# Projections of a two-block transformer kernel in a new order of weight panels

## The reference

```python
h = rms_norm(x, g_attn)                       # x: 1 x 512 x 1024
z = h @ w_in
(fq, fk, fv, f_logit, nq, kc, vc, ksl, vsl, kwn, vwn, n_gate, g_a, g_b) = split(z)   # 512,512,512,8,512,6 x 128,24,1024,1024
log_f = log_sigmoid(f_logit + b_f);  c = cumsum(log_f)          # bias of the first attention ("fox")
kc = silu(blocks(kc) @ w1_k) @ w2_k;  vc = silu(blocks(vc) @ w1_v) @ w2_v   # compressed keys and values
gates = sigmoid(n_gate)                       # three gates a head for the second attention ("nsa")
```

## Time and profile before

| | us |
|---|---|
| median of 3 runs | 1747.6 (1747.34 to 1747.71) |
| the profiled execution's own time | 1747.78 |
| its span in the trace | 1746.0 |
| TensorE (PE) busy, share of the span | 1648.7, 94% |
| first matmul starts | 13.63 |
| first matmul of the attention stage starts | 183.25 |

### The profile page before, as it was taken

How to read it: one execution, slowest core, us unless ns; L and a number is a source line. 1 busy time by engine, 2 the same in 40 slices (tenths; PEclk the granted TensorE clock), 3 DMA queues, 4 the chain that set the end, 5 groups by cost and what they waited for, 6 DMA issues and landing times.

```text
span 1746.0 us, 22108 instructions
## 1 busy us (share of the span) xinstructions
PE 1648.7 (94%) x7980; PEld 1350.3 (77%) x7980; DVE 1118.8 (64%) x1764; ACT 715.6 (41%) x1231; POOL 163.9 (9%) x187
## 2 busy tenths in 40 slices
PE   6979888998999999999989999999899899999997
PEld 5867676665887888888877787888678888888886
DVE  6465588886666666663578379998665644444456
ACT  5234686565343232322344234444633432232232
POOL 0001310000030000000000990000000000000000
PEclk9989899998999999999999999999999999999998
DMA  4326751111264555542213321221242233333332
GB/s 157 95 78 188 164 120 47 40 61 37 84 240 169 169 203 180 188 164 82 81 54 121 97 73 55 61 56 55 73 126 73 86 96 96 96 96 96 97 96 96
DMA packets 49825, 185.43 MB, mean 106 GB/s; under 512 B 6912, under 2 KB 9216, under 8 KB 47312
## 3 DMA queue, kind: packets, MB, share of 16 engines
q1 hardware_dynamic: 39456, 136.76, 24.8%
q0 software_dynamic: 10288, 47.60, 9.4%
HBM read 172.23 MB, written 6.85 MB: 103 GB/s over the span
## 4 chain that ended last, share of the span: by engine, by line
PE 68%; DVE 14%; ACT 4%; issue 3%; DMA 0%; ACTq 0%; DVEq 0%; SPq 0%
PE ps L1967 17%; PE ps L1969 16%; PE ps L1968 16%; DVE w_lo L1160 1%; PE ps L2369 1%; PE ps L2370 1%; PE ps L2371 1%; PE ps L2203 1%; PE ps L2204 1%; PE ps L2205 1%; PE ps L2164 1%; ACT w_hi L648 1%; PE ps L2426 1%; PE ps L2189 1%; PE ps L2144 1%
## 5 line engine op out<-in xcount | busy, mean ns | idle before, releaser
L1967 PE MATMUL ps<-h_hi,w_hi 128*128 128x512 f32 x1024 | 408.1, 399 | 34.0 <-DVE w_lo L1183 13.6
L1969 PE MATMUL ps<-h_hi,w_lo 128*128 128x512 f32 x1024 | 401.3, 392 | 0.0
L1968 PE MATMUL ps<-h_lo,w_hi 128*128 128x512 f32 x1024 | 401.1, 392 | 0.0
L1160 DVE TENSOR_TENSOR w_lo<-raw,w_hi 128x1024 fp32r<-128x1024 f32 x169 | 213.3, 1265 | 98.2 <-ACT w_hi L648 79.5
L1967 PEld LDWEIGHTS ps<-h_hi,w_hi 128*128 128x128 f32 x1024 | 193.9, 189 | 82.6 <-DVE w_lo L1183 13.6
L1968 PEld LDWEIGHTS ps<-h_lo,w_hi 128*128 128x128 f32 x1024 | 193.9, 189 | 41.3 <-issue 2.2
L1969 PEld LDWEIGHTS ps<-h_hi,w_lo 128*128 128x128 f32 x1024 | 193.6, 189 | 40.9
L581 ACT ACTIVATE w_hi<-raw 128x1024 fp32r<-128x1024 f32 x129 | 135.5, 1051 | 170.0 <-DMA raw<-in_panels 163.8
L1967 PE MATMUL ps<-f_hi,w_hi 128*128 128x512 f32 x408 | 166.8, 409 | 0.0
L1969 PE MATMUL ps<-f_hi,w_lo 128*128 128x512 f32 x408 | 161.3, 395 | 0.0
L1968 PE MATMUL ps<-f_lo,w_hi 128*128 128x512 f32 x408 | 161.0, 395 | 0.0
...
## 6 DMA issues: line engine op xcount, KB each, us to landing
raw<-in_panels SPq DMA_DIRECT2D x252, 512.0 KB, 3.5
...
X<-in_x SPq DMA_DIRECT2D x4, 512.0 KB, 7.7
...
```

Source lines behind the costliest of these rows:

```text
L1160: dve.tensor_tensor(w_lo[:, n % RING], raw[:, n % RING], w_hi[:, n % RING].bitcast(F32), ALU.subtract)\
L1967: pe.matmul(out, w_hi[:, u, b, :], hi[:, k, :N], start=start, stop=False)
L1968: pe.matmul(out, w_hi[:, u, b, :], lo[:, k, :N], start=False, stop=False)
L1969: ins = pe.matmul(out, w_lo[:, u, b, :], hi[:, k, :N], start=False, stop=stop)
```

## The change

All 32 first panels become one group `proj` in an order given by name: compressed keys and values first (in PSUM banks 2 and 3 of their own), the fox queries and keys, then values, compression panels (`c0` to `c7`), `low` (forget columns 0 to 7 and gate columns 32 to 55 in one panel), selected and windowed keys `s0`, `s1`, their values `v4`, `v5`, and the nsa queries `n0` to `n3`. The last, `none`, is a panel of zeros that is loaded and never multiplied. The block work of the compressed tensors is cut into pieces, one for each step (`BETWEEN`). x is loaded in five parts, the first of 256 KB; the square sums follow the split of h instead of alternating with it; activation tables are touched early. `blk_raw` is L1231's instruction, `blk_place` L1236's two, `blk_low` L1240's, `proj_low` the low part.

```diff
-GROUPS = [("fox_qk", 8), ("fox_v", 4), ("nsa_a", 4), ("mix", 16), ("gate", 16), ("branch", 8),
+GROUPS = [("proj", 32), ("gate", 16), ("branch", 8),
           ("out", 8)]
 for _c in range(4):
     GROUPS += [(f"ff1_{_c}", 8), (f"ff2_{_c}", 8)]
...
+PROJ = ["kc", "vc", "q0", "q1", "q2", "q3", "k0", "k1", "k2", "k3", "c0", "v0", "v1", "c1", "v2", "v3", "c2", "low",
+        "s0", "c3", "s1", "v4", "c4", "v5", "n0", "c5", "n1", "c6", "n2", "c7", "n3", "none"]
+AT = {name: n for n, name in enumerate(PROJ)}
+EVAC = [name for name in PROJ[2:] if name[0] in "qkvsn" and name != "none" or name == "low"]
+ORDER = {name: e for e, name in enumerate(EVAC)}
+SPLITS = [name for name in EVAC if name[0] in "qksn"]
+BANK = {name: e % 2 for e, name in enumerate(EVAC)}
+BANK.update({"kc": 2, "vc": 3, "n2": 4, "n3": 5})
+TMP_OF = {name: BANK[name] for name in EVAC}
+TMP_OF["n2"] = 1
+TURN_AFTER = {"v1": 0, "v2": 1, "v3": 2, "low": 3, "v5": 4, "n0": 5}
+NONE = AT["none"]
...
+    zf = place("zf", [8, T], F32, x_at)
+    gate_v = place("gate_v", [24, T], F32, x_at + T)
+    sig_n = place("sig_n", [24, T], F32, x_at + 2 * T)
+    nq_v = place("nq_v", [P, T], F32, cmp_at)
...
-        for f in range(4):
-            sp.dma_start(X[:, 2 * f:2 * f + 2, :], a["x"][:, 2 * f:2 * f + 2, :]).then_inc(in_x[f], 16)
-            if f == 0:
+        for n, (f, g) in enumerate(X_PARTS):
+            sp.dma_start(X[:, f:g, :], a["x"][:, f:g, :]).then_inc(in_x[n], 16)
...
-                gp.wait_ge(used, done(BASE["mix"] + 15))
+                gp.wait_ge(used, done(AT["c7"]))
...
+        def first_hi(m):
+
+            act.wait_ge(landed[m], 16)
+            act.activation(w_hi[:, m], raw[:, m], ACT.Copy).then_inc(hi_ready, 1)
+
+        act.wait_ge(setup, 1)
+        act.activation(row_max[:, 0, 0:1], p_cmp[0][:, 0, 0:1], ACT.Copy)
         act.wait_ge(in_v, 16)
         for f in range(KT):
-            act.wait_ge(in_x[f // 2], 16)
+            act.wait_ge(in_x[X_PART_OF[f]], 16)
             act.activation(h_hi[:, f, :], X[:, f, :], ACT.Copy, scale=vcol("g_attn", f)).then_inc(n_hi, 1)
+            if f == 0:
+                first_hi(0)
+        first_hi(1)
+        for f in range(KT):
             act.wait_ge(n_acc, f - 1) if f > 1 else None
             act.activation(tmp_v[:, f % 2, :], X[:, f, :], ACT.Square).then_inc(n_sq, 1)
-            if f in (2, 7):
-                m = 0 if f == 2 else 1
-                act.wait_ge(landed[m], 16)
-                act.activation(w_hi[:, m], raw[:, m], ACT.Copy).then_inc(hi_ready, 1)
-        panel_hi(2)
+            if f == 3:
+                first_hi(2)
+        first_hi(3)
         act.wait_ge(in_c, 16)
+        act.activation(row_max[:, 0, 0:1], eps, ACT.Sqrt)
...
+        for n, name in enumerate(PROJ[2:], 2):
+            if n + AHEAD == NONE + 1:
+                act.wait_ge(landed[NONE % RING], 16 * (NONE // RING + 1))
+                act.sem_inc(hi_ready, 1)
+            if n + AHEAD != NONE:
+                panel_hi(n + AHEAD)
+            if name == "n3":
+                act.wait_ge(sem("nsa_q_low"), 2)
+                fox_bias(0)
+                cmp_sums(1)
+            if name in SPLITS:
+                proj_high(name)
+            if name in TURN_AFTER:
+                v_out(TURN_AFTER[name])
+            if name == "k0":
+                blk_high(0)
+            if name == "v2":
+                blk_high(1)
+            if name == "k3":
+                act.activation(cst_r[:, 0:P], cst[:, C_ID:C_ID + P], ACT.Copy).then_inc(setup, 1)
+                act.activation(cst_r[:, P:2 * P], cst[:, C_MASK:C_MASK + P], ACT.Copy).then_inc(setup, 1)
+            if name == "low":
+                act.wait_ge(sem("forget_z"), 1)
+                chain(act.activation(lf_a[:], zf[:], ACT.Abs))
+                chain(act.activation(lf_a[:], lf_a[:], ACT.Exp, scale=-1.0))
+                act.activation(lf_a[:], lf_a[:], ACT.Ln, bias=cst[0:8, C_ONE:C_ONE + 1]).then_inc(sem("forget_ln"), 1)
+                act.wait_ge(sem("proj_val"), ORDER["low"] + 1)
+                act.activation(sig_n[:], gate_v[:], ACT.Sigmoid).then_inc(sem("gate_n"), 1)
+            if name == "s1":
+                cmp_sums(0)
+            if name == "c4":
+                cmp_hidden(0)
+            if name == "c5":
+                act.wait_ge(sem("cmp_k_out"), 1)
+                act.activation(kc_hi[:], ps[:, 6, P:P + 2 * CW].rearrange("p (g c) -> p g c", g=2), ACT.Copy)\
+                   .then_inc(sem("kc_hi_done"), 1)
...
+            if f == 3:
+                panel_lo(2)
+        panel_lo(3)
...
+        def proj_value(name):
+
+            dve.wait_ge(used, done(AT[name]))
+            dve.tensor_tensor(tmp_of(name), ps[:, BANK[name], :], rs1[:], ALU.mult).then_inc(sem("proj_val"), 1)
...
+        BETWEEN = {"q0": lambda: blk_raw(0, 0), "q1": lambda: blk_raw(0, 1), "q2": lambda: blk_raw(0, 2),
+                   "q3": lambda: blk_raw(0, 3), "k0": lambda: blk_place(0), "k1": lambda: blk_low(0),
+                   "k2": lambda: blk_raw(1, 0), "k3": lambda: blk_raw(1, 1), "v0": lambda: blk_raw(1, 2),
+                   "v1": lambda: blk_raw(1, 3), "v2": lambda: blk_place(1), "v3": lambda: blk_low(1)}
+
+        for n, name in enumerate(PROJ[2:NONE], 2):
+            if n + AHEAD == NONE + 1:
+                panel_lo(NONE + 1, also=1)
+            elif n + AHEAD != NONE:
+                panel_lo(n + AHEAD)
+            if name == "low":
+                dve.wait_ge(used, done(n))
+                dve.tensor_tensor(zf[:], ps[0:8, BANK[name], :], rs1[0:8, :], ALU.mult).then_inc(sem("forget_val"), 1)
+                dve.tensor_tensor(gate_v[:], ps[32:56, BANK[name], :], rs1[32:56, :], ALU.mult).then_inc(sem("proj_val"), 1)
+                dve.wait_ge(sem("forget_val"), 1)
                 dve.tensor_scalar(zf[:], zf[:], bf[:, 0:1], None, ALU.add).then_inc(sem("forget_z"), 1)
+            elif name in EVAC:
+                proj_value(name)
+            if name in BETWEEN:
+                BETWEEN[name]()
+            if name in SPLITS and name != "n3":
+                proj_low(name)
+            if name in TURN_AFTER:
+                v_out(TURN_AFTER[name])
...
+            if name == "s0":
                 dve.wait_ge(sem("forget_z"), 1)
                 dve.wait_ge(sem("forget_ln"), 1)
                 chain(dve.scalar_tensor_tensor(zf[:], zf[:], 0.0, lf_a[:], ALU.min, ALU.subtract))
                 chain(dve.tensor_scalar(zf[:], zf[:], -S8, None, ALU.mult))
                 chain(dve.memset(lf_a[:], 1.0))
                 dve.tensor_tensor_scan(cum[:], lf_a[:], zf[:], 0.0, ALU.mult, ALU.add).then_inc(sem("c_summed"), 1)
...
+            if name == "v4":
                 dve.wait_ge(sem("c_turned"), 1)
                 dve.tensor_scalar(c_q8[:], ps[:, 4, 0:32].rearrange("p (t h) -> p t h", h=8), -1.0, None, ALU.mult)\
                    .then_inc(sem("c_q_ready"), 1)
...
                 dve.wait_ge(sem("gate_turned"), 1)
                 dve.tensor_copy(gate_t[:], ps[:, 5, 0:96].rearrange("p (t h) -> p t h", h=24)).then_inc(sem("gate_t_ready"), 1)
...
+            if name == "n1":
                 dve.wait_ge(sem("kc_hi_done"), 1)
                 dve.tensor_tensor(kc_lo[:], ps[:, 6, P:P + 2 * CW].rearrange("p (g c) -> p g c", g=2), kc_hi[:].bitcast(F32),
-                                  ALU.subtract)
...
+                proj_low("n3")
+                panel_lo(BASE["gate"] + 1)
...
+        def project(n, out, ready=False, inside=None):
+
+            pe.wait_ge(lo_ready, n + 1)
+            for k in range(KT):
+                if ready:
+                    pe.wait_ge(n_lo, k + 1)
+                hi, lo = w_hi[:, n % RING, k, :], w_lo[:, n % RING, k, :]
+                pe.matmul(out, hi, h_hi[:, k, :], start=k == 0, stop=False, skip_group_check=True)
+                pe.matmul(out, hi, h_lo[:, k, :], start=False, stop=False, skip_group_check=True)
+                ins = pe.matmul(out, lo, h_hi[:, k, :], start=False, stop=k == KT - 1, skip_group_check=True)
+                if inside is not None and k == 2:
+                    inside()
+            ins.then_inc(used, 1)
+
+        def first_sum():
+
+            pe.wait_ge(in_c, 16)
+            pe.wait_ge(n_acc, KT)
+            pe.matmul(ps[:, 4, :], ones, sq_acc[:], start=True, stop=True, skip_group_check=True).then_inc(n_sum, 1)
...
+        for n, name in enumerate(PROJ[:NONE]):
+            if name[0] == "c":
                 compress(n)
             else:
-                panel(n // RING, n % RING, "mix", ps[:, r % 2, :], ALL, h_hi, h_lo, free=free)
...
+            if name == "q1":
+                rel_table()
+            if name in TURN_AFTER:
+                turn_v(TURN_AFTER[name])
+            if name == "s1":
+                turn_c()
+                turn_gate()
+            if name == "v4":
                 fold(0)
+            if name == "n0":
...
+                pe.wait_ge(bank_free, n + 2) if g else None
```

(69 more changed lines are left out.)

255 lines of the change are left out of this document (79 added, 176 removed).

## The result

| us | before | after | change |
|---|---|---|---|
| median of the runs shown together | 1747.65 (4 runs, 1747.34 to 1749.61) | 1728.55 (4 runs, 1725.58 to 1731.71) | -19.1 |
| profiled span | 1746.0 | 1729.9 | -16.1 |

The ratio of after to before is 0.9884, 95% interval [0.9866, 0.9902]; the forecast was 1729.3. The profiled execution (1731.71 us) is the slowest of the four, so its trace shows 3 us less gain than the median.

A forecast was written before the change was run, and what follows sets the result against it. TensorE, busy 94% of the span, was taken as the bound. The terms summed to -18.3 us, from the profiled 1747.78 to 1729.5, or 1729.3 as median; own range 1723 to 1734, with rivals 1720 to 1739.

The forecast's parts named there:

- one panel less: Projections: `low` replaces two panels and `none` has no matmuls, so 24 matmuls fewer on TensorE's path, -5.5 us.
- the start: First matmul moves from 13.63 to 9.9 us, needing only the first split and the panel's landing: -3.7 us.
- block work spread: Compressed tensors' VectorE work split over full-panel steps: the waits of 7.2 and 0.7 and 2.6 of clock go, -10.5 us.
- forget and gate, new wait: Before `s1`, TensorE waits 3.8 us behind ScalarE's table loads and panel rounding, plus 2.0 of clock: +5.8 us.
- w2 close behind: After `v5`, w2 is loaded nearer its use; `w2v` lands late and TensorE waits: +0.9 us (0 to 4).
- the tail: Before `n2`, a load slowed by POOL's burst again makes a wait near 2.9 and 1.7 behind it: 0 change.
- into the attention: At `fold(1)`, wait falls from 2.9 to 1.5 us and half of 3.3 lost clock returns: -3.0 us.
- everything later moves as it stands: After the first attention step, the gain stays whole because no load there is tied to wall-clock time: 0 change.
- Rival 4: Attention stage: the shift is lost waiting for VectorE, giving 1732.3 us; chance 0.71 jointly with the forecast.
- rival 1: Before `s1`, w2 and at the tail: the new waits stay away, 11.3 us faster, 1718.0 us; chance 0.13.
- 2: Tail: the ring starves, three loads of 8.6 us instead of one, +9.4, giving 1738.7 us; chance 0.12.
- Rival 3: Tail: store and bias starve the ring worse; at loads of 13 us, 22.4 more, 1751.7 us; chance 0.04.

The follow-up runs named there:

- e7: Changed kernel with the empty panel rounded and multiplied too, 24 matmuls more: 1731.13 us, ratio 0.99.
- e9: Changed kernel with the old start (x in four parts, squares alternating with splits, first panel rounded later, no early table loads): 1730.03 us, ratio 0.9902.
- e4: Changed kernel with the block work in two lumps, keys' in step k0 and values' in step v2: 1733.42 us, ratio 0.9919.
- e2: Changed kernel with ScalarE rounding s1's panel ahead of the forget and gate activations: 1726.83 us, ratio 0.9881.
- e1: The changed kernel run again, unedited; base of the later comparisons: 1727.13 us, ratio 0.9885.
- e5: Changed kernel with only head 0's 320 KB store to scratch_r moved early, behind the rows of r: 1721.81 us, ratio 0.9841.
- e6: Changed kernel with ScalarE's and VectorE's panel rounding ahead of the forget chain, and two turns moved behind v4: 1723.39 us, ratio 0.9853.
- e10: e8 with head 1's store to scratch_r also moved early, beside head 0's: 1719.22 us, ratio 0.9835.
- e8: Changed kernel with the edits of e5 and e6 together: 1717.78 us, ratio 0.9821.
- e3: Changed kernel with all eight 320 KB stores to scratch_r issued early, near 46 us: 1752.51 us, ratio 1.0027.

## Why the prediction was right, by its steps

| term | forecast | measured |
|---|---|---|
| one panel less | -5.5 | 4.9 by trace at `w2v`, 4.0 in medians (e7) |
| the start | -3.7 | 13.63 to 10.17: -3.5; undone alone +2.9 (e9) |
| block work spread | -10.5 | all its waits gone; lumped again, in other places, +6.3 (e4) |
| forget and gate, old waits | -2.3 | gone |
| forget and gate, new wait | +5.8 (3.8 + 2.0) | wait 3.99; from 112.21 to the turn 8.5, 3.0 over a panel |
| w2 close behind | +0.9 | 0 |
| the tail | 0 | wait 4.09 for 2.93, panel 7.1 as 7.2: +1.2 |
| into the attention | -3.0 | wait 0.63 for 2.9; first step 6.05 for 8.48: -4.7 |

The panel and the waits that are gone counted in full, the terms add up to -5.5 - 3.5 - 10.5 - 2.3 + 7.0 + 0 + 1.2 - 4.7 = -18.3 by the `w2v` product; the trace has 18.7 there (191.7 to 173.0). That this is the forecast's own sum is in part luck: the tail and the new wait came out 2.4 dearer, the attention and w2 2.6 cheaper. And the forecast let everything later move as it stands, which it does not (see "Later").

*Start.* Forecast 9.9, measured 10.17, 9.96 and 9.81. The reciprocal was forecast to end at 29.9 and ended at 31.0, and no bank waited for it; VectorE kept up through all eight query and key panels.

*The new wait before `s1`* was forecast at 3.8 and came as 3.99, 3.97 and 3.99, by the chain named: three table loads, the Sigmoid, then `w_hi`. The added clause, that a running sum would fill the time if the clock were full, is what e2 shows: without the wait TensorE stood 1.94 for `cum` and 0.47 for `w_lo`. *On the tables, the Trainium skill ("ScalarE: Activation LUTs", "What ACT_TABLE_LOAD costs") adds a drain of some 1380 ns to each load of 1283 ns; the rows of after have loads of 1.28 us with the next activation 0.01 to 0.02 behind each, and the wait is 3.99, not the 3.8 + 4.1 that an estimate from the page's figures would give.*

*The price of a wait.* The forecast added 2.0 of clock to a wait of 3.8 and 1.7 to one of 2.9. Measured behind `s1`'s wait: 3.0 in the first trace, 1.7 in e1 (110.70 to the turn at 117.94), 3.1 in e5; behind `n2`'s wait 1.6 and 1.7 in the first two, 2.7 in e2, e4 and e6. So the same wait in the same kernel cost 1.7 in one execution and 3.0 in another. Waits of 2.4 together (e2) and of 2.0 (e10) were each followed by 1.7; the wait of 1.9 for `gate_z` in the first attention head was followed by matmuls of 0.63 us before and of 0.39 after. Behind waits up to 0.8 us (e8) the granted clock stayed 1.00.

*w2.* The forecast took 5.2 us for `w2v` to land and a wait of 0.9; the load took 3.6 in after, and there was no wait. Ahead of the store it stands in both kernels; but before, SyncE issued a panel load 0.3 us behind it, and after, the next panel load comes 4.8 us behind. That this is what made the 5.2 was not tested.

*Tail and attention.* The wait before `n2` was put at 2.9 for a load of 8.6; the load took 9.7 and the wait was 4.09. The forecast blamed the burst as a whole; e5 shows that it is the one store. The step into the attention was sized too small: with 0.63 the wait fell under those that keep the clock, so all of the loss there went, not half.

*Later.* Of the 18.7, 16.1 were left at the end of the first trace, and this step of the prediction ("everything later moves as it stands") is wrong by 1.4 us. These go at the start of group `out`, where TensorE waits for the reloaded X. The reload in the kernel before, in the changed one and in e7, and TensorE's wait in the changed one:

```profile
X<-in_x POOLq DMA_DIRECT2D x1, 2048.0 KB, 8.2
...
X<-in_x POOLq DMA_DIRECT2D x1, 2048.0 KB, 9.7
...
X<-in_x POOLq DMA_DIRECT2D x1, 2048.0 KB, 8.3
...
472.45 0.47 PE L1996 MATMUL ps<-h_hi,w_hi 128*128 128x512 f32 x1 [1.29 <-DVE X L1468]
```

It is no chance: in all ten traces with one panel less the load takes 9.4 to 9.8 us and TensorE waits 1.07 to 1.39; in the kernel before and in e7, which has the extra panel, it takes 8.2 and 8.3 and there is no wait. So it goes with the panel less, which brings 4.9 to 5.5 at its place and 4.0 at the end. Why the load takes longer there stays open. The other loss of the first trace, 1.1 near the second block's first norm (granted clock 0.50 from 880 to 885 us, 1.00 in e1), did not come again: of the other ten traces seven win 1.5 to 1.8 there on the one of the kernel before, which has a slow stretch of its own at that place (granted clock 0.80 from 900 to 905 us), and three win nothing. So in e1 21.8 were won at `w2v`, 20.3 near 830 us and 22.3 at the end. Rival 4 (a loss in the attention stage) did not hold: from the `w2v` product to group `out` no trace differs from the kernel before by more than 1.7 us, in both directions.

*Rivals.* 1 was wrong: the waits before `s1` and `n2` came. Take both away, as e8 does, and the kernel runs 1717.8, where rival 1 said 1718.0; that is close in part by luck, since its 11.3 holds 0.9 for a wait before the `w2k` product that never came, and e8 is 9.3 under e1. 2 and 3 (the ring starves) did not hold for after, and e3 shows the mechanism of 3 in force: loads of 35 us, and a time above the kernel before. Rival 3's own formula gives 28.2 - 4.6 = 23.6 at L = 13, and so 1752.9, not 22.4 and 1751.7; and it takes 7.7 us of TensorE's work where the tail's term takes 8.4. By the two a load of 8.6 costs 5.0 or 4.3, where the prediction uses 4.6 and 4.7. The forecast doesn't hang on it.
